# Overflow lists between the first pairs, the norm's weights in the copies and the sample last in the router, slot sums as gather columns, the count read early

## The reference

```python
x = x + einsum(mixed, w_out)
h = rmsnorm(x, g_ffn_norm)
logits = h @ w_router + b_router
top_vals, top_idx = top_k(logits, 4)          # of 32 experts
gates = softmax(top_vals)
# per chosen expert e:
hg = h @ w_gu[e] + b_gu[e]                    # 1024 -> 2048
g, up = minimum(hg[:, 0::2], 7), clip(hg[:, 1::2], -7, 7)
y = ((up + 1) * g * sigmoid(1.702 * g)) @ w_dn[e] + b_dn[e]
x = x + sum(gate * y)
```

## Time and profile before

| | |
|---|---|
| median of 3 runs | 1111.6 us (1110.28 to 1112.56) |
| profiled execution | 1111.7 us |
| its span, first to last instruction | 1109.8 us |
| mean granted PE clock | 0.985 |
| busy share of the span | PE 94%, DVE 29%, ACT 14%, POOL 5% |
| DMA | 421.75 MB, 380 GB/s over the span |

### The profile page before, as it was taken

One profiled execution on the slowest core, in us unless ns is written; L12 is line 12 of the kernel. 1 busy time (PEld: TensorE's weight loads), 2 busy tenths in 40 slices (PEclk: granted clock), 3 DMA queues, 4 the chain that ended last, 5 costly groups with the idle time before them and its releaser, 6 DMA issues.

```text
span 1109.8 us, 13158 instructions
## 1 busy us (share of the span) xinstructions
PE 1043.6 (94%) x5125; PEld 438.7 (40%) x5125; DVE 322.1 (29%) x652; ACT 150.3 (14%) x279; POOL 56.0 (5%) x88
## 2 busy tenths in 40 slices
PE   6999788999999999999999999999999999999996
PEld 4686363343434333333242424333333333242432
DVE  1482578213131313131213131313131221213132
ACT  2246231010101010101010101010101101010100
POOL 5164110000000000000000000000000000000000
PEclk9999888999999999999999999999999999999999
DMA  9921558699999999999999999999999999999992
GB/s 342 294 103 40 227 197 335 283 427 429 428 427 425 428 429 427 428 428 428 428 429 427 430 428 427 430 428 426 430 428 427 430 428 428 430 427 427 427 426 116
DMA packets 33452, 421.75 MB, mean 380 GB/s; under 512 B 4514, under 2 KB 5010, under 8 KB 8702
## 3 DMA queue, kind: packets, MB, share of 16 engines
q1 hardware_dynamic: 31918, 418.34, 90.1%
q0 software_dynamic: 1264, 2.75, 0.8%
q10 hardware_dynamic: 240, 0.25, 0.1%
HBM read 420.06 MB, written 2.33 MB: 381 GB/s over the span
## 4 chain that ended last, share of the span: by engine, by line
PE 60%; DMA 34%; DVE 4%; ACT 1%; issue 1%; SPq 0%; DVEq 0%; ACTq 0%
DMA ring<-in_w_gate_up_dram 30%; PE ps L1631 22%; PE ps L1657 13%; PE ps L1541 6%; PE ps L1261 3%; PE ps L1238 3%; DMA regA<-in_w_down_dram 3%; PE ps L1673 2%; PE ps L1439 2%; PE ps L1639 2%; PE ps L1264 2%; PE ps L1600 1%; PE ps L1547 1%; PE ps L1724 1%; DVE bd L1137 0%
## 5 line engine op out<-in xcount | busy, mean ns | idle before, releaser
L1631 PE MATMUL ps<-ring,regA 128*64 128x512 f32 x1536 | 340.5, 594 | 27.4 <-DMA ring<-in_w_gate_up_dram 27.1
L1631 PEld LDWEIGHTS ps<-ring,regA 128*64 128x64 f32 x1536 | 107.9, 137 | 254.9 <-issue 200.3
L1657 PE MATMUL ps<-ring,regA 128*64 128x512 f32 x736 | 166.3, 601 | 0.1
L1178 DVE TENSOR_SCALAR regA<-ps 128x512 f32<-128x512 f32 x32 | 22.1, 691 | 431.6 <-PE ps L1639 431.6
L711 ACT ACTIVATE regA<-regA 128x512 f32<-128x512 f32 x32 | 20.2, 630 | 662.7 <-DVE regA L1178 662.7
L1192 DVE COPY regA<-ps 64x512 f32<-64x512 f32 x60 | 41.3, 689 | 190.3 <-PE ps L1657 189.4
L1657 PEld LDWEIGHTS ps<-ring,regA 128*64 128x64 f32 x736 | 50.8, 138 | 101.9 <-issue 94.7
L1673 PE MATMUL ps<-regA 128*128 128x512 f32 (+1 forms) x136 | 70.9, 647 | 0.0
L1541 PE MATMUL ps<-regA 128*128 128x256 f32 x256 | 65.5, 400 | 1.7 <-DVE regA L1068 1.7
L1631 PE MATMUL ps<-regX,regA 128*64 128x512 f32 x256 | 58.2, 596 | 4.5 <-DMA regX<-in_w_gate_up_dram 3.9
L1631 PE MATMUL ps<-regA 128*64 128x512 f32 x256 | 57.6, 592 | 0.0
(11 more groups left out here) (297 smaller groups left out, 724.3 us busy)
## 6 DMA issues: line engine op xcount, KB each, us to landing
ring<-in_w_gate_up_dram SPq DMA_DIRECT2D x96, 2048.0 KB, 31.4
ring<-in_w_down_dram SPq DMA_DIRECT2D x48, 2048.0 KB, 35.2
regX<-in_w_gate_up_dram SPq DMA_DIRECT2D x16, 2048.0 KB, 30.8
regA<-in_w_gate_up_dram SPq DMA_DIRECT2D x16, 2048.0 KB, 30.1
regA<-in_w_down_dram SPq DMA_DIRECT2D x8, 2048.0 KB, 35.0
regX<-in_w_down_dram SPq DMA_DIRECT2D x7, 2048.0 KB, 35.7
regA<-in_w_in_dram SPq DMA_DIRECT2D x8, 896.0 KB, 12.1
ring<-in_w_out_dram SPq DMA_DIRECT2D x2, 1024.0 KB, 33.8
```

Of the source, the lines that this page charges most:

```text
L1631: mm = pe.matmul(ps[64 * h:64 * h + 64, 1 + n, :], xT[:, kt, 64 * odd:64 * odd + 64], w[:, c:c + 512], start=(kt == 0), stop=False)
L1657: mm = pe.matmul(ps[64 * n:64 * n + 64, 0, :], actT[:, j, 64 * h:64 * h + 64], w[:, 1024 * j + 512 * n:1024 * j + 512 * n + 512], start=(h ...
```

## The change

- **Lists.** The code of the overflow lists becomes three functions. DVE runs them inside the first two pairs, each before the second activation; these two pairs are written out ahead of DVE's loop.
- **Router order.** It is `RSEQ = (0, 1, 2)`: the sample comes last in the top-four chain, the counts and the gather. PE's output products are reordered with it: half (1,0), transposes of tile 0, half (1,1), quarters. The logits use three banks.
- **Norm's weights.** The gathered rows hold only x times 1/rms, made by three ACT operations. The weights lie as one value per partition (`gft`, 4 KB, one DMA) and multiply when the gathered, transposed rows are copied: `copy_x` is eight ACT copies of 128x128 with a scale, and the first gate/up starts with the first of them. DVE's and POOL's products go.
- **Slot sums.** The three columns stand behind the rows (`WIDE = D + 3`), so the gather's last quarter is 259 columns wide and `slot_sums` goes from the pairs. DVE copies them from bank 7 once ACT has copied the rows. The first pair keeps its own `slot_sums`, which with the transposes of the gates moves into the middle of its first gate/up (`first_gates`).
- **Loads.** Load 6 is issued after the last state transposes (before: last of all), load 7 after the second of the three logits.
- **Count.** PE reads the overflow count before the last pair.

```diff
-            sp.wait_ge(S["kr_tr"], 1)
-            sp.wait_ge(S["qbd_r"], 2)
-            sp.dma_start(gf_bc, a["g_ffn_norm"].to_broadcast([P, D])).then_inc(s_gf, 16)
...
+            sp.dma_start(gft.rearrange("p (k t) -> p k t", t=2),
+                         a["g_ffn_norm"][0].rearrange("(k p t) -> p k t", p=P, t=2)).then_inc(s_gf, 16)
...
             load_first(3)
+            sp.wait_ge(S["st_tr"], 3)
+            load_first(6)
             sp.wait_ge(S["out_r"], 5)
             load_first(2)
-            sp.wait_ge(S["logit"], NT)
+            sp.wait_ge(S["logit"], 2)
             load_first(7)
-            sp.wait_ge(S["xn"], 1)
-            sp.wait_ge(S["xw"], 3)
-            sp.wait_ge(S["st_tr"], 3)
-            load_first(6)
...
-            then(pool.tensor_tensor(xnq, xq[:, :], gf_q, ALU.mult), "xw")
...
+            def scale_f(i):
+                dst, src = (xnq[:, 0:D // 4], xq[:, :]) if i == 2 else (xn_row[:, i, 0:D], x_row[:, i, :])
+                then(act.activation(dst, src, ACT.Copy, scale=small[:, 40 + i:41 + i]), "xn1")
 
             square_f(0, 0)
             square_f(0, 1)
-            copy_f(0)
+            copy_f(0, 0)
             root_f(0)
+            square_f(1, 0)
+            scale_f(0)
+            square_f(1, 1)
+            root_f(1)
+            scale_f(1)
+            copy_f(1, 0)
+            copy_f(1, 1)
...
             def copy_x(g, half):
                 act.wait_ge(m_xtr, 2 * g + (half + 1))
-                act.activation(xT[:, 4 * half:4 * half + 4, :],
-                               ps[:, XBANK[half], :].rearrange("p (k t) -> p k t", k=4), ACT.Copy).then_inc(m_xT, 1)
+                for j in range(4):
+                    kt = 4 * half + j
+                    act.activation(xT[:, kt, :], ps[:, XBANK[half], P * j:P * j + P], ACT.Copy,
+                                   scale=gft[:, kt:kt + 1]).then_inc(m_xT, 1)
...
             add_r(0, 1, 2)
-            dve.wait_ge(S["out_r"], 3)
-            add_quarters(4, rs_r, "xq")
+            add_r(1, 0, 3)
             copy_f(0)
             mean_f(0)
-            add_r(1, 0, 4)
+            add_r(1, 1, 4)
+            dve.wait_ge(S["out_r"], 5)
+            add_quarters(4, rs_r, "xq")
+            mean_f(1)
+            top4(0)
             copy_q()
-            mean_f(1)
-            norm_0()
-            top4(0)
             top4(1)
-            add_r(1, 1, 5)
+            mean_f(2)
             places(0)
             places(1)
-            copy_f(1)
-            mean_f(2)
             top4(2)
             places(2)
...
             def slots_of(g):
-                dve.wait_ge(m_ix, g + 1)
-                dve.tensor_copy(idxg, ps[:, 5, 0:3]).then_inc(m_idx, 1)
+                dve.wait_ge(m_xr, g * 2 + 2)
+                dve.tensor_copy(idxg, ps[:, 7, 256:259]).then_inc(m_idx, 1)
...
                 place_gates(p)
+                for part in between:
+                    part()
                 activate(p * 2 + 1)
...
-            slots_of(0)
+            dve.wait_ge(S["gt_tr"], 1)
+            dve.tensor_copy(idxg, ps[:, 7, 256:259]).then_inc(m_idx, 1)
             dve.wait_ge(s_tok, 32)
-            with dve.Fori(0, PAIRS - 1) as p:
+            pair(0, True, (over_counts, lambda: over_half(0)))
+            pair(1, True, (lambda: over_half(1), over_list))
+            with dve.Fori(2, PAIRS - 1) as p:
                 pair(p, True)
...
-            out_quarters(yg, 1, 4, "out_r")
+            out_half(1, 0, yg, 1, 2, "out_r")
...
-            out_half(1, 0, yg, 1, 2, "out_r")
+            out_half(1, 1, yg, 1, 3, "out_r")
+            out_quarters(yg, 1, 4, "out_r")
+            pe.wait_ge(S["wr_g"], 1)
+            pe.wait_ge(S["xq"], 4)
+            logits(0)
+            pe.wait_ge(S["xmid"], 3)
+            x_transposes_f(1, 0, 2)
+            pe.wait_ge(S["xmid"], 4)
+            x_transposes_f(1, 1, 3)
...
+            def first_gates():
+                pe.wait_ge(m_oh, 4)
+                slot_sums()
+                for i in range(NT):
+                    mm = transpose(ps[0:E, 0, P * i:P * i + ROWS[i]], gate_cols[0:ROWS[i], i, 0:E], ROWS[i])
+                mm.then_inc(S["gt_tr"], 1)
...
                 for kt in range(KT):
-                    if first and kt % 4 == 0:
-                        pe.wait_ge(m_xT, kt // 4 + 1)
+                    if first:
+                        pe.wait_ge(m_xT, kt + 1)
+                    if first and kt == 4:
+                        first_gates()
...
             pair(PAIRS - 2, PAIRS // 2 - 1, 0, True)
-            pair_last()
             pe.wait_ge(S["ovd"], 1)
             n_over = pe.value_load(ovi[0:1, 0:1], min_val=0, max_val=N_OVER // 2)
+            pair_last()
```

More of the change, by code:

```diff
@@ L34 @@
 SEQ = (0, 2, 1)
+RSEQ = (0, 1, 2)
 HD = 64
@@ L676, in _ @@
             square_f(0, 1)
-            copy_f(0)
+            copy_f(0, 0)
             root_f(0)
+            square_f(1, 0)
[5 more added lines that the diff above has]
+            copy_f(1, 1)
             act.wait_ge(S["xq"], 8)
             then(act.activation(sq_f[:, 0:D // 4], xq[:, :], ACT.Square, accum_out=small[:, 38:39]), "ss_f")
[L681 to L689, removed]
-            copy_f(1)
-            square_f(1, 1)
             root_f(2)
-            scale_f(1, 3)
+            scale_f(2)
             exp_top(0)
@@ L1121, in over_e, with over_counts, over_half @@
                 return row[:, None, :].to_broadcast([P, 8, E])
-            for h in range(2):
+            def over_counts():
+                then(dve.tensor_scalar(ext, cnt, float(CAP), None, ALU.is_gt))
+                for j in range(2, -(-T // CAP)):
+                    then(dve.scalar_tensor_tensor(out=ext, in0=cnt, scalar=float(CAP * j), in1=ext,
+                                                  op0=ALU.is_gt, op1=ALU.add))
+                then(dve.tensor_tensor_scan(incl, ext, ext, 0.0, ALU.add, ALU.bypass))
+                then(dve.tensor_tensor(excl, incl, ext, ALU.subtract))
+            def over_half(h):
                 r8 = slice(8 * h, 8 * h + 8)
@@ L1192, in copy_y, with pair @@
                     dve.tensor_copy(y_sb[n][64 * odd:64 * odd + 64, :], ps[64 * n:64 * n + 64, 0, :]).then_inc(m_ysb, 1)
-            def pair(p, ahead):
+            def pair(p, ahead, between=()):
                 if ahead:
@@ L1513, in _, with count_before @@
             for h in range(2):
-                transpose(ps[:, 1, P + P * h:2 * P + P * h], xq[:, P * h:P * h + P], P)
-            pe.wait_ge(S["ss_f"], 3)
-            pe.matmul(ps[:, 1, 16:17], cc("same"), small[:, 38:39], start=True, stop=True).then_inc(S["xq_tr"], 1)
-            pe.wait_ge(S["wr_g"], 1)
-            logits(0)
+                mm = transpose(ps[:, 1, P + P * h:2 * P + P * h], xq[:, P * h:P * h + P], P)
+            mm.then_inc(S["xq_tr"], 1)
+            logits(1)
+            pe.wait_ge(S["ss_f"], 5)
+            pe.matmul(ps[:, 3, 16:17], cc("same"), small[:, 38:39], start=True, stop=True).then_inc(S["xq_tr"], 1)
             logits_sample()
-            pe.wait_ge(S["xmid"], 3)
-            x_transposes_f(1, 0, 2)
-            out_half(1, 1, yg, 1, 3, "out_r")
             msk = oht[:, 0:96].rearrange("p (i e) -> p i e", i=NT)
-            def count_before(k):
-                i = SEQ[k]
-                pe.wait_ge(S["mask"], k + 1)
-                for m in range(k + 1):
-                    j = SEQ[m]
+            def count_before(i):
+                for j in range(i + 1):
                     if i != j:
@@ new lines, in count_before, with quarter, gather_tile @@
+                    mm = pe.matmul(ps[:, LBANK[i], 0:E], lhs, msk[0:ROWS[j], j, :], start=(j == 0), stop=(i == j))
+                mm.then_inc(S["posd"], 1)
+            def quarter(j, wide):
+                return 256 * j, 256 * j + (259 if wide and j == 3 else 256)
+            def gather_tile(j, i, stop, wide=True):
+                n0, n1 = quarter(j, wide)
+                return pe.matmul(ps[:, QBANK[j], 0:n1 - n0], oneh[:, i, :], xn_row[:, i, n0:n1],
+                                 start=(i == 0), stop=stop)
@@ L1563, in _ @@
             count_before(2)
-            pe.wait_ge(S["xn1"], 2)
+            pe.wait_ge(S["xn1"], 3)
             pe.wait_ge(m_oh, 3)
             for j in range(4):
-                mm = gather_tile(j, 1)
+                mm = gather_sample(j, True, False)
                 if j % 2:
                     mm.then_inc(m_xg, 1)
-            for m, j in enumerate(SEQ):
+            for j in range(NT):
                 mm = pe.matmul(ps[:, 3, 0:E], cc("ones", 0, ROWS[j]), msk[0:ROWS[j], j, :],
-                               start=(m == 0), stop=(m == NT - 1))
+                               start=(j == 0), stop=(j == NT - 1))
```

140 lines of the change are left out of this document (57 added, 83 removed).

## The result

The changed kernel takes 1104.02 us (median of five runs, 1102.56 to 1106.01) beside 1111.6 us before; the ratio is 0.9941 [0.9927, 0.9954]. By this ratio it is 0.59% faster (the two medians alone differ by 7.6 us, 0.68%) where 1.15% was forecast. That is inside the range given, and close to the time of rival (a), 1104.8. The profiled execution took 1105.86 us, at the slow end of its five runs, with a span of 1103.9 us.

A forecast was written before the change was run, and what follows sets the result against it. The prediction took the DMA stream of expert weights to bound the kernel. Its terms, 2.1 + 9.9 + 0.9 = 12.9 us earlier, went against 1111.7 us and gave 1098.8 us, with a range of 1094.5 to 1105.

The forecast's parts named there:

- rival (a): Clock falls in the first placing even without a pause: 6.9 us gained together, 1104.8 us; chance 0.20.
- What bounds the kernel: Expert-weight DMA is the limit; each microsecond the stream's restart (202.06 us) moves is a microsecond of the end.
- rival (e): Something else fills the DMA hole and the end doesn't move with the restart: only the tail, 1110.8 us; chance 0.04.
- Rival (d): Clock falls before the gathers, stays at 1.2 GHz through first gate/up: 5.0 us slower, 1116.7 us; chance 0.03.
- Term 2: First pair, gate/up to the DMA stream's restart: 34.67 us now, 24.78 new, so 9.9 us earlier.
- Term 1: Router up to first gate/up: 2.1 us earlier, bounds 3.1 earlier to 1.9 later, half a gather allowed for low clock.
- Term 3: Tail: count read before the last pair moves the 3.80 us branch, 0.9 us earlier.
- rival (c): Tail branch is short once its register is old: 15.8 us gained together, 1096.0 us; chance 0.07.
- At nothing: Eight row copies, slot sums as gather columns, POOL and DVE products, gain's one DMA, loads' places: no gain expected.

The follow-up runs named there:

- e1: Changed kernel with the first pair's bias placing contracted over 128 rows instead of 32, the added rows zeros: 1099.58 us, ratio 0.9888 to the kernel before.
- e2: Changed kernel with four unread 512-column matmuls on PE, two before the second logits and two after the sample's logits: 1100.7 us, ratio 0.9895.
- e3: Changed kernel with the overflow lists back on DVE ahead of the first pair: 1111.4 us, ratio 0.9999 to the kernel before.
- e7: e6 plus unread matmuls: two in the wait before the second logits, five in the wait ahead of the first output products: 1091.67 us, ratio 0.9834.
- e8: Changed kernel with two 512-column row copies per pair instead of eight, norm's weights left out: 1104.5 us, ratio 0.9940 to the kernel before.
- e9: Changed kernel with the edits of e3 and e1 together, lists back and first placing over 128 rows: 1106.32 us, ratio 0.9961.
- e4: Changed kernel with the overflow count read after the last pair again: 1107.09 us, ratio 0.9952 to the kernel before.
- e5: Changed kernel with the edits of e1 and e2 together: 1097.25 us, ratio 0.9869 to the kernel before.
- e6: e1 with tile 0's count, places and gather moved ahead of tile 1's top four: 1098.63 us, ratio 0.9881 to the kernel before.

## Why the prediction was right about the sign and wrong about the size

**What bounds the kernel: right.** From the fifth refill to the end takes 907.0 to 907.6 us in the changed kernel, `e1`, `e2`, `e3`, `e7`, `e8` and `e9`, whose refills lie between 184.10 and 204.23 us; in `e4` it is 908.1, for the later count, and in `e5` and `e6` 908.6, where the last placings took 5.40 us instead of 3.70. So each microsecond of the restart was a microsecond of the end, and rival (e) is out. Rival (d) is out too: gate/up ran its first 32 matmuls in 7.09 us, full speed.

**Term 2 is the step that failed**: "I take 9.9, since no pause is left and the nearest undisturbed rows are the later pair's". The pause did go, and gate/up to placing took 16.34 us (forecast 16.25). But the clock fell in the first placing without it, so placing to down took 7.74 instead of 4.65 and down to refill 6.02 instead of 3.88: 5.2 us of the 9.9 stayed. The rows taken as a model differ in one thing that stood in them: a later pair places 128 rows (`128*8`), the first 32 (`32*8`). `e1` changes that (POOL's zeroing is over long before) and gets 24.88 us where 24.78 were forecast. Rival (a), with 0.20, named this outcome, and set its cost at 4.9. That the whole time lies so near to that of (a) is in part luck: the router gave 0.2 us where (a) had 1.0, and the tail 2.6 where it had 0.9.

**Term 1 was mis-sized.** The low clock was foreseen and its cost set at 1.0 us, "half a gather"; it cost about 3.4: the second logits took 3.18 instead of 1.97, the gathers 5.90 instead of 3.70, as most of both gathers ran at 1.2 GHz too. Without that the 31.09 us from start to gate/up would have been about 27.7 (estimate), where the full-clock sum of the forecast was 28.2. `e9`, whose logits ran at the full clock and whose gathers didn't, fits: 29.87, which is 2.2 more. `e2` gets 28.29 and not 27.7 because its second fill costs some 0.6, as DVE's wait in `e5` shows: its gathers start 20.34 us after the router's start, those of `e9`, without a fill, 19.71. So the nearness of 28.29 to the forecast's 28.2 is partly chance. The bound of 1.9 later allowed for more than the clock cost.

**Term 3: right in mechanism, small in size.** The early count is worth 0.9 in the trace of `e4`, as forecast; the branch kept about its length, so rival (c) is out. The whole tail gave 2.6: the branch was 0.4 shorter in this execution, and the eight last placings kept the full clock (1.6). The 1.6 was a bound, not the forecast, and it is not the early count's: with the late count (`e4`) they take 3.70 too. Whether any of the change's edits earned it isn't shown.

The Trainium skill, Runtime: NRT & Kernel Launch, Instruction fetch mechanics, has a taken branch outside the fetched window wait for its code. The branch of 3.38 to 3.90 us in ten traces, against 0.08 to 0.24 for the loop's, agrees with it; no run here shows what the branch waited for. The Trainium skill, Advanced Engine Details and Errata, Control Flow Timing, has compare-and-branch at about 108 ns; that does not hold for this branch.

**At nothing: right.** The lists (`e3` against the change: 7.3 us if they stay, 2.50 us to spare where they went), the eight copies (376 ns each, forecast 0.37; `e8`). Not tried by themselves: the slot sums as gather columns, the gain's one DMA, the loads' places and the products taken from POOL and DVE; the sums of `e5` leave them at most some tenths of a microsecond on the path.

**What stays open.** Why the last placings ran at the full clock in the changed kernel and not in the kernel before: the pauses ahead of them don't sort the runs (2.39 us in `e4` and 3.70 for eight placings, 1.81 in `e6` and 5.40). Why the clock fell later in the first placing of `e2`. Which of the two fills in the router was needed: `e2` and `e5` have both, `e7` has the first alone, with a gather where the second stood, and all three kept the clock.

## What to carry to other kernels

Where a forecast takes rows of another stretch as its model, compare the shapes in them, the contracted rows too: a matmul over 32 rows took as long as one over 128 at the same clock, but the clock then fell behind it. A PE wait that lies on the path can be worth filling with matmuls that nobody reads, and a short contraction padding with zeros: the two edits together took this change from 0.9941 to 0.9869. Try a shorter chain again after the clock is mended, as the same reordering gained nothing at 1.2 GHz and about 0.8 us (estimate) at 2.4. A fill that later work must wait for costs time: the second one here cost some 0.6 us (estimate).

## What the runs showed of the hardware that was not expected

The clock fell to 1.2 GHz while PE was busy 13.00 of 13.00 us, during and behind placings over 32 rows, and stayed at 2.4 GHz behind the same matmuls padded to 128 rows (0.61 and 1.00 in 186 to 199 us). The Trainium skill, TensorE: Matmul & The Clock Gate, Why this matters for your kernels, puts such drops down to gaps in which PE idles; `e9` bears that out for a pause of 5.88 us, but the changed kernel's first placing had none. The same section has a single matmul over few rows take as long as one over 128; here eight took 0.61 and 0.62 us.

After a wait of 1.89 us ahead of sixteen narrow matmuls the clock was at 1.2 GHz for the next 10 us or so (152.29 to about 163); with two matmuls of 512 columns in that wait and two more behind the sample's logits it stayed at 2.4 GHz. In `e9` the logits behind a wait of 1.88 us took 1.97, full speed, and the gathers behind them 5.90: behind the same wait the clock fell sooner in one execution and later in another.
